# Forgetting attention: a 64-row score matmul and a 16-row gate matmul become 128-row matmuls over zeroed rows

## The reference

```
q = heads(q_raw) * (FOX_DH ** -0.5)
k = heads(k_raw)
v = heads(v_raw)
log_f = jax.nn.log_sigmoid(f_raw.astype(f32) + f_bias.astype(f32))
cum = jnp.cumsum(log_f, axis=1).transpose(0, 2, 1)
...
    logits = jnp.einsum('bhtd,bhsd->bhts', qb, k) + (cb[..., :, None] - cum[..., None, :])
    logits = jnp.where(mask, logits, NEG_INF)
    p = jax.nn.softmax(logits, axis=-1)
    return jnp.einsum('bhts,bhsd->bhtd', p, v)
```

## Time and profile before

| | us |
|---|---|
| median of 3 runs | 1591.63 |
| lowest, highest | 1587.15, 1592.59 |
| span of the profiled execution | 1584.7 |

### The profile page before, as it was taken

One profiled execution on the slowest core, in us unless ns is written; L12 is line 12 of the kernel. 1 busy time (PEld: TensorE's weight loads), 2 busy tenths in 40 slices (PEclk: granted clock), 3 DMA queues, 4 the chain that ended last, 5 costly groups with the idle time before them and its releaser, 6 DMA issues.

```text
span 1584.7 us, 17694 instructions
## 1 busy us (share of the span) xinstructions
PE 1476.8 (93%) x6975; PEld 1160.8 (73%) x6975; DVE 1023.8 (65%) x1357; ACT 759.1 (48%) x999; POOL 121.8 (8%) x143
## 2 busy tenths in 40 slices
PE   7899989989989999999999998999999799999981
PEld 5777668668767788888888787886648688888871
DVE  4888884564336555455646557746454799888976
ACT  5453353654334322223224543244455778888763
POOL 0500000000000010000000303200000101111012
PEclk9999999899999999999999999999999899999996
DMA  5212232202202432232213221110005699999975
GB/s 206 82 62 80 80 112 102 80 20 87 80 27 93 147 135 73 100 118 94 90 56 125 90 80 63 71 54 27 27 1 199 221 419 412 410 407 415 407 305 186
DMA packets 39330, 231.58 MB, mean 146 GB/s; under 512 B 4400, under 2 KB 5696, under 8 KB 17104
## 3 DMA queue, kind: packets, MB, share of 16 engines
q1 hardware_dynamic: 30640, 200.09, 33.6%
q0 software_dynamic: 7648, 27.87, 4.7%
q10 hardware_dynamic: 960, 2.49, 0.5%
HBM read 213.66 MB, written 16.78 MB: 145 GB/s over the span
## 4 chain that ended last, share of the span: by engine, by line
PE 76%; DVE 11%; ACT 6%; issue 4%; DMA 2%; POOL 0%; POOLq 0%; ACTq 0%; DVEq 0%
PE bank L445 15%; PE bank L446 14%; PE bank L447 14%; PE bank L3014 5%; PE bank L3016 5%; PE bank L3015 5%; PE bank L591 3%; DVE w_lo L372 2%; PE bank L464 1%; PE bank L2264 1%; PE bank L465 1%; PE bank L466 1%; ACT w_hi L366 1%; PE bank L2243 1%; PE bank L2009 1%
## 5 line engine op out<-in xcount | busy, mean ns | idle before, releaser
L445 PE MATMUL bank<-h_hi,w_hi 128*128 128x512 f32 x952 | 387.9, 407 | 10.9 <-DVE w_lo L372 8.0
L446 PE MATMUL bank<-h_lo,w_hi 128*128 128x512 f32 x952 | 377.0, 396 | 0.0
L447 PE MATMUL bank<-h_hi,w_lo 128*128 128x512 f32 x952 | 376.9, 396 | 0.0
L372 DVE TENSOR_TENSOR w_lo<-w_raw,w_hi 128x2048 fp32r<-128x2048 f32 (+3 forms) x86 | 188.9, 2196 | 91.5 <-ACT w_hi L366 90.9
L445 PEld LDWEIGHTS bank<-h_hi,w_hi 128*128 128x128 f32 x952 | 180.8, 190 | 63.4 <-DVE w_lo L372 10.9
L447 PEld LDWEIGHTS bank<-h_hi,w_lo 128*128 128x128 f32 x952 | 180.4, 190 | 42.0
L446 PEld LDWEIGHTS bank<-h_lo,w_hi 128*128 128x128 f32 x952 | 181.0, 190 | 40.6 <-issue 2.2
L366 ACT ACTIVATE w_hi<-w_raw 128x2048 fp32r<-128x2048 f32 (+3 forms) x87 | 154.6, 1777 | 63.5 <-PE bank L447 63.5
L3199 DVE TENSOR_TENSOR h_lo<-w_raw,h_hi 128x2048 fp32r<-128x2048 f32 x32 | 73.1, 2291 | 12.2 <-ACT h_hi L3100 12.2
L3199 DVE TENSOR_TENSOR lo_b<-raw_b,hi_b 128x2048 fp32r<-128x2048 f32 x32 | 73.1, 2287 | 7.2 <-ACT hi_b L3100 7.2
L446 PE MATMUL bank<-a_lo,w_hi 128*128 128x512 f32 x176 | 69.0, 392 | 0.0
(11 more groups left out here) (582 smaller groups left out, 2832.9 us busy)
## 6 DMA issues: line engine op xcount, KB each, us to landing
w_raw<-in_params_dram SPq DMA_DIRECT2D x122, 1024.0 KB, 5.0
raw_b<-in_params_dram SPq DMA_DIRECT2D x51, 1024.0 KB, 8.3
w_raw<-in_params_dram SPq DMA_DIRECT2D x16, 704.0 KB, 4.1
result_rows<-osb POOLq DMA_DIRECT2D x16, 512.0 KB, 8.2
result_rows<-prm POOLq DMA_DIRECT2D x8, 512.0 KB, 3.2
xt<-in_x_t_dram POOLq DMA_DIRECT2D x1, 2048.0 KB, 9.3
scratch_rows<-htm SPq DMA_DIRECT2D x4, 512.0 KB, 3.0
out_dram<-pr SPq DMA_DIRECT2D x4, 512.0 KB, 2.6
```

The costliest lines, as they stand in the source:

```text
L372: V.tensor_tensor(k.w_lo[:, g % SPLIT, 0:size], k.raw[:, g % RAW, 0:size], k.w_hi[:, g % SPLIT, 0:size].bitcast(F32), ALU.subtract).then_i ...
L445: PE.matmul(ps, wh, hi[:, c, 0:width], start=c == 0, stop=False)
L446: PE.matmul(ps, wh, lo[:, c, 0:width], start=False, stop=False)
L447: m = PE.matmul(ps, wl, hi[:, c, 0:width], start=False, stop=c == parts - 1)
```

## The change

- `fq` is no longer one tile [128, 4, 512] but two tiles [128, 2, 2, 512], the second in the place of the HGRN2 values. For each block of two heads it holds two versions: in the first, rows 64 to 127 are zero, in the second rows 0 to 63.
- `dve_queries` writes both versions with two instructions. The constant factor 1/8 becomes a column of the new tile `one_head`, which is 1/8 on the rows of one head and 0 on the others.
- `ncum` and `sel2` get 128 rows; POOL clears them, and makes `one_head`, at the head of `pool_mix`. DVE fills the first 16 rows of `ncum` as before. The fill of the 16 x 8 corner of `sel2` moves from the start of `dve_mix_in` to behind the low parts of the first query slot, and waits for POOL (`fx_zero`).
- The score matmul reads all 128 rows of queries and keys: the other head's keys meet zeros. The gate matmul reads all 128 rows of `sel2` and `ncum`: rows 16 to 127 are zero in both.

```diff
-        self.w0, self.fq, self.w1, self.fk = h("w0", [P, 4 * T]), h("fq", [P, 4, T]), h("w1", [P, 4 * T]), h("fk", [P, 4, T])
+        self.w0, fqa, self.w1, self.fk = h("w0", [P, 4 * T]), h("fqa", [P, 2, 2, T]), h("w1", [P, 4 * T]), h("fk", [P, 4, T])
...
+        fqb = Memory(nc, sq_at, m.at)("fqb", [P, 2, 2, T])
+        self.fq = [(fqa, fqb)[blk // 2][:, blk % 2, :, :] for blk in range(4)]
...
-        self.ncum = m("ncum", [2 * FX_H, T], F32R)
+        self.ncum = m("ncum", [P, T], F32R)
...
-        self.sel2 = m("sel2", [2 * FX_H, FX_H], F32R)
+        self.sel2, self.one_head = m("sel2", [P, FX_H], F32R), m("one_head", [P, 2])
...
 def dve_queries(k, stage, b, out):
...
     V.wait_ge(s.gemm, i + 1)
-    V.scalar_tensor_tensor(out, k.bank[i % 4][:, :], HD ** -0.5, k.rs[:, :], ALU.mult, ALU.mult).then_inc(s.evac_v, 1)
+    v(V.scalar_tensor_tensor(out[:, 0, :], k.bank[i % 4][:, :], k.one_head[:, 0:1], k.rs[:, :], ALU.mult, ALU.mult))
+    V.scalar_tensor_tensor(out[:, 1, :], k.bank[i % 4][:, :], k.one_head[:, 1:2], k.rs[:, :], ALU.mult, ALU.mult).then_inc(s.evac_v, 1)
...
     G.wait_ge(s.n_rs, NORM["final"] + 1)
+    g(G.memset(k.sel2[:, :].bitcast(F32), 0.0))
+    g(G.memset(k.one_head[:, :], 0.0))
+    g(G.memset(k.ncum[:, :].bitcast(F32), 0.0))
+    g.own()
+    g(G.memset(k.one_head[0:HD, 0:1], HD ** -0.5))
+    G.memset(k.one_head[HD:P, 1:2], HD ** -0.5).then_inc(s.fx_zero, 1)
+    G.wait_ge(s.fx_zero, 1)
     g(G.memset(k.hs[:, :, :, :], 0.0))
...
-    v(V.tensor_tensor(k.sel2[:, :], k.ident[0:2 * FX_H, 0:FX_H], k.ident[0:2 * FX_H, FX_H:2 * FX_H], ALU.add))
     V.wait_ge(s.n_rs, NORM["final"] + 1)
...
     dve_split_to(k, SLOT0["fqa"])
+    V.wait_ge(s.fx_zero, 1)
+    v(V.tensor_tensor(k.sel2[0:2 * FX_H, :], k.ident[0:2 * FX_H, 0:FX_H], k.ident[0:2 * FX_H, FX_H:2 * FX_H], ALU.add))
     dve_keys(k, 0)
     V.wait_ge(s.fx_cum, 2)
-    V.tensor_copy(k.ncum[:, :], k.bank[6][0:2 * FX_H, :]).then_inc(s.fx_ncum, 1)
+    V.tensor_copy(k.ncum[0:2 * FX_H, :], k.bank[6][0:2 * FX_H, :]).then_inc(s.fx_ncum, 1)
...
-            PE.matmul(ps, k.fq[r0:r0 + HD, blk, t * P:t * P + P], k.fk[r0:r0 + HD, blk, 0:n], start=True, stop=False, tile_position=(r0, 0))
-            PE.matmul(ps, k.sel2[:, h:h + 1].broadcast_to([2 * FX_H, P]), k.ncum[:, 0:n], start=False, stop=True).then_inc(s.sm_s, 1)
+            PE.matmul(ps, k.fq[blk][:, h % 2, t * P:t * P + P], k.fk[:, blk, 0:n], start=True, stop=False)
+            PE.matmul(ps, k.sel2[:, h:h + 1].broadcast_to([P, P]), k.ncum[:, 0:n], start=False, stop=True).then_inc(s.sm_s, 1)
```

More of the change, by code:

```diff
@@ L47 @@
     pads_zero ff_conv ff_silu ff_x
-    fx_consts fx_turn fx_act fx_dve fx_cum fx_ncum fx_o fx_oc
+    fx_consts fx_zero fx_turn fx_act fx_dve fx_cum fx_ncum fx_o fx_oc
     gn_sq gn_sum gn_rs gn_out
@@ L1758, in dve_queries @@
 def dve_queries(k, stage, b, out):
-    V, s = k.nc.vector, k.s
+    V, v, s = k.nc.vector, k.v, k.s
     i = BLOCK0[stage] + b
     V.wait_ge(s.gemm, i + 1)
-    V.scalar_tensor_tensor(out, k.bank[i % 4][:, :], HD ** -0.5, k.rs[:, :], ALU.mult, ALU.mult).then_inc(s.evac_v, 1)
+    v(V.scalar_tensor_tensor(out[:, 0, :], k.bank[i % 4][:, :], k.one_head[:, 0:1], k.rs[:, :], ALU.mult, ALU.mult))
+    V.scalar_tensor_tensor(out[:, 1, :], k.bank[i % 4][:, :], k.one_head[:, 1:2], k.rs[:, :], ALU.mult, ALU.mult).then_inc(s.evac_v, 1)
 def in_two(x):
@@ L2193, in dve_hgrn @@
         if l < 2:
-            dve_queries(k, "fqa", l, k.fq[:, l, :])
+            dve_queries(k, "fqa", l, k.fq[l])
         elif l < 4:
@@ L2209, in dve_hgrn @@
     dve_split_to(k, SLOT0["fkb"])
-    dve_queries(k, "fqb", 0, k.fq[:, 2, :])
+    dve_queries(k, "fqb", 0, k.fq[2])
 KEY_STEPS = range(0, 8)
@@ L2255, in pe_fox @@
             h, t = i // TT, i % TT
-            r0, blk, n = HD * (h % 2), h // 2, FX_WIDTHS[i]
+            blk, n = h // 2, FX_WIDTHS[i]
             if i >= 2:
@@ L2404, in dve_fox @@
         if step == 0:
-            dve_queries(k, "fqb", 1, k.fq[:, 3, :])
+            dve_queries(k, "fqb", 1, k.fq[3])
             V.wait_ge(s.gn_rs, 1)
```

## The result

| | median us | lowest to highest |
|---|---|---|
| before, in the same session | 1592.11 | 1587.15 to 1592.80 |
| after | 1577.54 | 1576.75 to 1578.18 |

The ratio is 0.992, with a 95% interval of 0.990 to 0.994: 9.4 to 15.6 us are saved. The medians differ by 14.6 us; 1578.5 was forecast.

What follows compares the result with a forecast made beforehand. PE's instruction order was taken to bound the attention loop. 16.4 us gross less 2.7 to softmax gave 13.7; less 0.6 on DVE, 13.1 saved from 1591.63, so 1578.5 us, range 1573 to 1586.

Steps and rivals of the forecast that it cites:

- The bound: In the forgetting-attention loop PE's instruction order sets the time; net saving there 13.7 us.
- 16.4 us gross: Row-count changes between PE matmuls in the loop vanish: 6.1 into score, 5.7 score to gate, 4.6 after the gate.
- 2.7 us back to softmax: Loop saving lost waiting for ACT's exponentials: 2 x 0.57 at steps 21 and 22, 1.1 at 25 and 26, 0.5 at 30.
- DVE +0.6, second query 0: Doubled query evictions on DVE in the other mixer's levels: the first adds 0.6 us, the second nothing under POOL's multiplication.
- Clock 1.00 in the loop: Sign of the forecast: PE's granted clock stays 1.00 throughout the attention loop.
- C: Rival, chance 0.04: PE's waits in the loop lower its clock seven times, making the run slower, 1598.1 us.
- A: Rival, chance 0.13: only some row-change costs in the loop go, saving 6.8 us, 1584.8 us.
- B: Rival, chance 0.06: the cost belongs to the operands, not rows; nothing saved, DVE adds 0.6 to 1.2, 1592.5 us.
- Later stages keep the gain: After the loop, all stages start from its last exponential and shift whole, keeping the loop's saving.

Runs made afterwards that it cites:

- e1: The changed kernel with the 16-row gate matmul put back and the full-row score kept; 1585.46 us, ratio 0.997 to the kernel before.
- e3: The changed kernel with score and gate matmul both on the head's 64 rows, odd heads losing the gate term; 1583.66 us, ratio 0.995.
- e2: The changed kernel with the 64-row score put back and the full-row gate matmul kept; 1585.83 us, ratio 0.998.
- e10: The changed kernel, unaltered, run and profiled once more; 1576.32 us, ratio 0.992, loop 83.10 us.
- e4: The changed kernel with both old matmuls (64-row score, 16-row gate) put back, keeping the double evictions and memsets; 1587.33 us, ratio 0.998.
- e9: The changed kernel with output-weight splits moved later on ACT and DVE, and query block 0 evicted after level 1; 1573.09 us, ratio 0.989.

## Why the prediction was right

- **The bound.** Right. The loop was PE's order, and 12.9 us of it are gone (96.02 to 83.10 at equal clock; 13.7 forecast).
- **16.4 us gross.** Right border by border: 0.19 into the score, 0.19 to the gate (0.14 forecast at 128 columns), 0.20 to what follows (0.15 behind a gate of 128 columns). e1, e3 and e2 show each by itself. The step leaned on one pair of rows, 0.86 beside 1.06 on one instruction, and they carried it.
- **2.7 us back to softmax.** Right in size and place, wrong in one cause. The table shows how much earlier than in before a score starts, each counted from the first score of its loop (e10, clock 1.00). A step gains 0.4 to 0.6 us where nothing holds it up. Between the scores of steps 20 and 22 nothing is gained, nor between 24 and 26, nor between 29 and 30: some 1.1, 1.1 and 0.6 us given back, where I put 1.1 (2 x 0.57), 1.1 and 0.5. The remaining 0.7 of the 3.5 us between 16.4 and 12.9 is in pieces of 0.1 to 0.2 us; one is the very first score, which adds 0.49 in both kernels.

| step of the score | 20 | 22 | 24 | 26 | 29 | 30 |
|---|---|---|---|---|---|---|
| earlier than before, us | 10.24 | 10.16 | 10.96 | 10.91 | 12.42 | 12.36 |

  At steps 21 and 22 PE waits for the exponential 1.88 us instead of 1.13, and at step 30 the score again starts when ACT is done, though the waits of PE don't list it, since the recorded durations of the turns cover it. In steps 24 and 25 it isn't the exponential, as I had it, but DVE's probabilities: the turns at 1151.14 and 1152.45 wait 0.58 and 0.21 us for them. I had carried only ACT's ends forward, and DVE's scaling is as late. From the chain of waits of after:

```profile
1151.91 0.50 DVE fp L2414
...
1152.45 0.66 PE bank L593 x4
...
1161.76 0.36 ACT fp L2335 x2
...
1162.16 0.91 PE bank L2275 x2
```

- **DVE +0.6, second query 0.** 0.7 and 0. The new form takes 0.75 us and adds 0.66 where I took 0.60 from the old one's 0.69. POOL's memsets and its wait push the memset that follows 0.96 us later, with 46.33 us of idling behind the masks. The start of the loop can't price these terms: e4's loop starts at 1084.8 and e10's at 1081.36.
- **Clock 1.00 in the loop.** Wrong, and the text said that a stretch under 0.95 would speak for C. A fall does occur, though from waits of 1.1 and 0.8 us, not the 2.5 from which I let C decide, because the only fall that I read stood behind one wait of 2.51. It comes once and not seven times, and only in some executions. It costs 1.6 us, near the 1.8 of clocks that C took from the earlier trace rows. C's mechanism is real; its price stays far below the gain.
- **A and B.** Out: no border keeps its price but those of the column count.
- **Later stages keep the gain.** Right within the jitter: 407.7 us from the loop's end before, 409.0 after, 407.3 to 409.3 in the others.

The agreement of 1578.5 with 1577.54 owes something to luck. What the profiles account for is 12.9 us in the loop less 0.7 in the levels, 12.2 in all at equal clock, and 10.6 in the execution of after whose clock fell; 13.1 were forecast. The medians differ by more: 14.6 us here, 13.7 in the second session (1590.06 against e10's 1576.32). Each kernel of the experiments, e4 with its unchanged loop included, likewise lies 1.6 to 5.0 us further under the median of before than its loop and its levels account for (an estimate, from one profile each). Where this remainder lies is open: the two profiled executions of before were quick ones, about 1585.9 and 1586.97 us against medians of 1590.0 to 1592.1, so no profile shows a usual one.

## What to carry to other kernels

Where PE sets the pace and short matmuls of different row counts alternate, read what each adds in the chain of waits, and compare one instruction behind two different predecessors: if it costs 0.2 us more behind a matmul of other rows, zero-padding to equal rows takes that away, three times a step here, and the extra rows cost nothing. Pay for the padding on an engine that has cover. When PE gets faster, look next at what the other engines have between the softmax pieces: moving one weight split took the loop from 83.10 to 81.24 us. Its median, 1573.2 us, is the fastest beside that of e9 (1573.1) among the kernels that leave nothing out; after had 1577.5 and 1576.3 in other sessions, so the lead rests on the loops more than on totals.

## What the runs showed that I had not expected

- The clock can fall after two short waits (1.09 and 0.79 us, with 1.4 us of matmuls between them), and the same waits leave it alone in another execution: 84.69 against 83.10 us for the same loop.
- A 64-row gate behind a 64-row score costs no border (0.23), so equal rows suffice; they need not be 128.
- A stationary narrower in columns costs 0.20 us behind it (0.43 against 0.23) and 0.14 ahead of it (2.30 against 2.16). The second shows only in the two steps whose weight load needn't wait for ACT (2.30 against 2.29 in the others).
- DVE's weight split stretches from 2.28 to 3.15 or 3.81 us by when it starts beside POOL's multiplication, and then ends 2.15 us after POOL. The Trainium skill, SBUF — State Buffer, "SBUF: two separate sides", describes the port pair that DVE and GpSimd share as an exclusive lock; the trace agrees for the split, which reads two tensors from SBUF, while the query evictions, which read PSUM, kept their 0.74 us beside the same POOL instruction.
